# Two half chunks of weights at a time: sixteen wide matmuls, then sixteen narrow ones, in a two-block transformer kernel

## The reference, cut to what matters

```python
def first_block(x, mem, ...):          # per layer
    h = rms_norm(x, norm_mix[l])
    z = h @ w_in[l]                    # 2048 x 5144, then gMLP, dilated and NSA attention
    x = x + jnp.concatenate([out_a, out_b, out_c], axis=-1) @ w_out[l]
    ...
    x = x + o @ xattn_wo[l]            # cross attention to 256 memory tokens
    h = rms_norm(x, norm_mlp[l])
    x = x + jnp.square(jax.nn.relu(h @ w_up[l])) @ w_down[l]      # 2048 x 8192 x 2048
    return rms_norm(x, final_norm)

def second_block(x, c, ctx, ...):
    h_lat = x * (1.0 + sc_m) + sh_m    # modulation, from silu(c) @ w_ada
    mix_lat, _ = _token_mixer(h_lat, h_ctx, ...)   # gated linear attention and pooling, w_in, w_gla_out, w_pool_out, w_out
    x = _layer_norm(DEEPNORM_ALPHA * x + gt_m * mix_lat, ...)
    ffn_lat = _swiglu(x * (1.0 + sc_f) + sh_f, w_ffn_in, w_ffn_out)   # 2048 x 11264, 5632 x 2048
    return _layer_norm(DEEPNORM_ALPHA * x + gt_f * ffn_lat, ...)
```

## Time and profile before

| | |
|---|---|
| median of 3 runs | 3040.98 us |
| lowest, highest | 3037.58, 3041.06 us |
| span of the profiled execution | 3038.4 us |
| PE busy | 2968.7 us (98%), 16590 matmuls |
| DVE busy | 2176.0 us (72%) |
| ACT busy | 1460.2 us (48%) |
| HBM read | 635.52 MB, 213 GB/s over the span |

### The profile page before, as it was taken

The page is one execution under the profiler, slowest core; times in us unless marked ns, Lnnn a source line. Parts: engine busy times, 40 slices in busy tenths (PEclk is TensorE's granted clock), DMA queues, the critical chain, the costliest instruction groups (busy, mean ns, idle before and its releaser), DMA issues.

```text
span 3038.4 us, 40261 instructions
## 1 busy us (share of the span) xinstructions
PE 2968.7 (98%) x16590; PEld 2552.0 (84%) x16590; DVE 2176.0 (72%) x2685; ACT 1460.2 (48%) x1953; POOL 8.5 (0%) x21
## 2 busy tenths in 40 slices
PE   8999999999999999999999999999999999999998
PEld 7888888888888888877887778888878888888887
DVE  5556767899899886677766666648888775555557
ACT  5345555544444445444544444544546444444444
POOL 0000000000000000000000000000000000000000
PEclk9999999999999999999999999999999999999999
DMA  6545244677677785566654445559556765555553
GB/s 250 194 166 207 99 139 143 235 272 260 249 273 265 289 314 197 192 230 241 248 211 171 171 168 190 202 217 345 215 179 232 287 244 193 187 188 192 184 193 111
DMA packets 106661, 648.60 MB, mean 213 GB/s; under 512 B 11856, under 2 KB 11856, under 8 KB 42352
## 3 DMA queue, kind: packets, MB, share of 16 engines
q1 hardware_dynamic: 99936, 621.86, 56.5%
q10 hardware_dynamic: 4608, 16.78, 1.4%
q0 software_dynamic: 1936, 7.41, 0.7%
HBM read 635.52 MB, written 10.49 MB: 213 GB/s over the span
## 4 chain that ended last, share of the span: by engine, by line
PE 92%; DVE 5%; ACT 2%; issue 1%; DMA 1%; SPq 0%; DVEq 0%; ACTq 0%
PE PS L510 50%; PE PS L515 26%; PE PS L551 3%; PE PS L553 3%; PE PS L558 3%; DVE RL L2084 1%; PE PS L1081 1%; PE PS L993 1%; PE PS L788 1%; ACT RH L1226 1%; PE PS L927 0%; PE PS L973 0%; DMA RW<-in_w_ckv 0%; PE PS L579 0%; PE PS L690 0%
## 5 line engine op out<-in xcount | busy, mean ns | idle before, releaser
L2084 DVE TENSOR_TENSOR RL<-RW,RH 128x1024 fp32r<-128x1024 f32 x974 | 1178.1, 1221 | 559.2 <-ACT RH L1226 552.7
L1226 ACT ACTIVATE RH<-RW 128x1024 fp32r<-128x1024 f32 x974 | 1015.5, 1055 | 780.8 <-PE PS L515 634.0
L510 PE MATMUL PS<-A,RH 128*128 128x512 f32 x4544 | 1163.4, 398 | 26.4 <-ACT RH L1226 10.1
L510 PEld LDWEIGHTS PS<-A,RH 128*128 128x128 f32 x4544 | 825.9, 191 | 188.3 <-issue 31.6
L515 PEld LDWEIGHTS PS<-A,RL 128*128 128x128 f32 x4544 | 624.8, 192 | 45.5
L515 PE MATMUL PS<-A,RL 128*128 128x256 f32 x4544 | 637.6, 283 | 0.0
L510 PE MATMUL PS<-H,RH 128*128 128x512 f32 x2304 | 581.9, 394 | 1.2 <-ACT RH L1226 1.2
L510 PEld LDWEIGHTS PS<-H,RH 128*128 128x128 f32 x2304 | 415.9, 189 | 76.7 <-issue 1.4
L515 PEld LDWEIGHTS PS<-H,RL 128*128 128x128 f32 x2304 | 314.7, 191 | 22.7
L515 PE MATMUL PS<-H,RL 128*128 128x256 f32 x2304 | 321.5, 282 | 0.0
L1233 ACT ACTIVATE LT<-PS 128x512 f32<-128x512 f32 x232 | 138.2, 596 | 326.9 <-PE PS L515 326.8
(11 more groups left out here) (256 smaller groups left out, 1560.0 us busy)
## 6 DMA issues: line engine op xcount, KB each, us to landing
RW<-in_w_fin SPq DMA_DIRECT2D x88, 1024.0 KB, 4.8
G<-in_w_ada SPq DMA_DIRECT2D x160, 512.0 KB, 5.9
RW<-in_w_up SPq DMA_DIRECT2D x64, 1024.0 KB, 4.9
RW<-in_w_down SPq DMA_DIRECT2D x64, 1024.0 KB, 5.1
RW<-in_w_fout SPq DMA_DIRECT2D x44, 1024.0 KB, 4.8
RW<-in_w_v SPq DMA_DIRECT2D x32, 1024.0 KB, 4.8
RW<-in_w_bg SPq DMA_DIRECT2D x32, 1024.0 KB, 4.8
RW<-in_w_k SPq DMA_DIRECT2D x16, 1024.0 KB, 4.8
```

The lines of the kernel that those rows point to most:

```text
L510: t.matmul(pair[mm][:, :], wh[:, k, mm * 128:mm * 128 + 128], x2(4 * c + k)[0], start=first and k == 0, stop=False, skip_group_check=True)
L1226: a.activation(m.high(x), m.slot(j)[:, x % 2 * HC:x % 2 * HC + HC], ACT.Copy).then_inc(s["hi"], 1)
L2084: v.tensor_tensor(m.low(x), m.slot(j)[:, x % 2 * HC:x % 2 * HC + HC], m.high(x).bitcast(F32), ALU.subtract).then_inc(s["lo"], 1)
```

## The change

In the calls of `outb`, `up`, `down`, `g2`, `pout`, `fin`, `fout` and `out2` (616 of the 974 halves) `gemm` gets `paired=True`: on each even turn it lists the wide matmuls of two halves, then the narrow ones of both; on the odd turn it lists no matmul of its own. The loop around it (the `beside` steps, the `yield`s, the other lanes) is as before. `outa`, `gout`, `xq` and the rest keep one half at a time. In all products the last wide matmul of a half raises a new semaphore `hused`, and ScalarE, before it overwrites a high buffer, waits for `hused` and `lo` of the half that lay there instead of `used`. What SyncE and the evacuations wait for is unchanged.

```diff
-        for b, c in steps(blocks, halves, zipped):
-            n = num.half
-            num.half += 1
+
+        def high(n, b, c):
+
             if c == 0:
                 block_begins(g0 + b)
             t.wait_ge(s["hi"], n + 1)
...
                 for mm in range(2):
-                    t.matmul(pair[mm][:, :], wh[:, k, mm * 128:mm * 128 + 128], x2(4 * c + k)[0], start=first and k == 0,
-                             stop=False, skip_group_check=True)
+                    done = t.matmul(pair[mm][:, :], wh[:, k, mm * 128:mm * 128 + 128], x2(4 * c + k)[0],
+                                    start=c == 0 and k == 0, stop=False, skip_group_check=True)
+            done.then_inc(s["hused"], 1)
+
+        def low(n, b, c):
+
             t.wait_ge(s["lo"], n + 1)
...
             done.then_inc(s["used"], 1)
+
+        order = steps(blocks, halves, zipped)
+        for x, (b, c) in enumerate(order):
+            n = num.half
+            num.half += 1
+            last = c == halves - 1
+            if not paired:
+                high(n, b, c)
+                low(n, b, c)
+            elif x % 2 == 0:
+                high(n, b, c)
+                high(n + 1, *order[x + 1])
+                low(n, b, c)
+                low(n + 1, *order[x + 1])
             if rest is not None:
                 next(rest, None)
             yield
...
             if x >= NR:
-                a.wait_ge(s["used"], x - NR + 1)
+                a.wait_ge(s["lo"], x - NR + 1)
+                a.wait_ge(s["hused"], x - NR + 1)
             a.activation(m.high(x), m.slot(j)[:, x % 2 * HC:x % 2 * HC + HC], ACT.Copy).then_inc(s["hi"], 1)
```

More of the change, by code:

```diff
@@ L105 @@
 SIGNALS = (
-    "hi", "lo", "used", "cmp", "lt",
+    "hi", "lo", "hused", "used", "cmp", "lt",
     "sil", "fh", "fl", "sq", "sqa", "rs",
@@ L489, in block_begins, with gemm @@
             t.wait_ge(m.pair[g % 2], g // 2)
-    def gemm(blocks, halves, x2, need, zipped=False, beside=None):
+    def gemm(blocks, halves, x2, need, zipped=False, beside=None, paired=False):
         rest, g0 = None, num.block
         num.block += blocks
-        for b, c in steps(blocks, halves, zipped):
-            n = num.half
-            num.half += 1
+        def high(n, b, c):
             if c == 0:
@@ L502, in gemm @@
             wh = m.high(n).rearrange("p (k n) -> p k n", k=4)
-            wl = m.low(n).rearrange("p (k n) -> p k n", k=4)
-            first, last = c == 0, c == halves - 1
             pair = m.banks[2 * ((g0 + b) % 2):2 * ((g0 + b) % 2) + 2]
@@ L509, in gemm @@
                 for mm in range(2):
-                    t.matmul(pair[mm][:, :], wh[:, k, mm * 128:mm * 128 + 128], x2(4 * c + k)[0], start=first and k == 0,
-                             stop=False, skip_group_check=True)
+                    done = t.matmul(pair[mm][:, :], wh[:, k, mm * 128:mm * 128 + 128], x2(4 * c + k)[0],
+                                    start=c == 0 and k == 0, stop=False, skip_group_check=True)
+            done.then_inc(s["hused"], 1)
+        def low(n, b, c):
             t.wait_ge(s["lo"], n + 1)
+            wl = m.low(n).rearrange("p (k n) -> p k n", k=4)
+            pair = m.banks[2 * ((g0 + b) % 2):2 * ((g0 + b) % 2) + 2]
             for k in range(4):
@@ L515, in gemm @@
                     done = t.matmul(pair[mm][:, 0:256], wl[:, k, mm * 128:mm * 128 + 128], x2(4 * c + k)[1], start=False,
-                                    stop=last and k == 3, skip_group_check=True)
+                                    stop=c == halves - 1 and k == 3, skip_group_check=True)
             done.then_inc(s["used"], 1)
+        order = steps(blocks, halves, zipped)
[11 more added lines that the diff above has]
+                low(n + 1, *order[x + 1])
             if rest is not None:
@@ L552, in gemm_n @@
                                  skip_group_check=True)
-                        t.matmul(out[mm], lo(2 * c + k)[:, rows[mm]], wh[:, k, :], start=False, stop=False,
-                                 skip_group_check=True)
+                        done = t.matmul(out[mm], lo(2 * c + k)[:, rows[mm]], wh[:, k, :], start=False, stop=False,
+                                        skip_group_check=True)
+                done.then_inc(s["hused"], 1)
                 t.wait_ge(s["lo"], n + 1)
@@ L578, in small @@
             for k in range(8):
-                t.matmul(bk.ap[:, :], wh[:, k, :], A2(8 * half + k)[0], start=half == k == 0, stop=False,
-                         skip_group_check=True)
+                done = t.matmul(bk.ap[:, :], wh[:, k, :], A2(8 * half + k)[0], start=half == k == 0, stop=False,
+                                skip_group_check=True)
+            done.then_inc(s["hused"], 1)
             t.wait_ge(s["lo"], n + 1)
@@ L871, in mix_of @@
         return need
[L873 removed]
+    L.outb = lambda: gemm(8, 2, twin(m.A, 8), mix_of(4), paired=True)
     L.fed_rest = lambda: None
@@ L931, in up @@
         first = q == b0 == 0
-        yield from gemm(2 * nb, 4, A2, fed(2) if first else nothing, zipped=first)
+        yield from gemm(2 * nb, 4, A2, fed(2) if first else nothing, zipped=first, paired=True)
     def down(q):
-        yield from gemm(8, 4, twin(m.H, 16 * q, 24), lambda c: t.wait_ge(s["ul"], 8 * q + c + 1))
+        yield from gemm(8, 4, twin(m.H, 16 * q, 24), lambda c: t.wait_ge(s["ul"], 8 * q + c + 1), paired=True)
     L.ada, L.up, L.down = ada, up, down
@@ L1149, in tensor_program @@
     L.p2, L.pool = p2, pool
-    L.g2 = lambda: gemm(8, 4, A2, nothing)
+    L.g2 = lambda: gemm(8, 4, A2, nothing, paired=True)
     L.gout = lambda: gemm(8, 4, H2, lambda c: t.wait_ge(s["gl"], c + 1))
-    L.pout = lambda: gemm(8, 2, A2, lambda c: t.wait_ge(s["pl"], c + 1))
+    L.pout = lambda: gemm(8, 2, A2, lambda c: t.wait_ge(s["pl"], c + 1), paired=True)
     L.cp_loads = lambda: idle(12)
@@ L1197, in fin @@
         first = b0 == 0
-        yield from gemm(2 * nb, 4, A2, (lambda c: t.wait_ge(s["fl2"], c + 1)) if first else nothing, zipped=first)
+        yield from gemm(2 * nb, 4, A2, (lambda c: t.wait_ge(s["fl2"], c + 1)) if first else nothing, zipped=first, paired=True)
     def fout(part, first, n):
         yield from gemm(8, n // 4, twin(m.H, first, 24), lambda c: t.wait_ge(s["fgl"], first // 2 + c + 1),
-                        beside=normed(1) if part == 2 else None)
-    L.out2 = lambda: gemm(8, 4, H2, lambda c: t.wait_ge(s["ml2"], 17 + c), beside=normed(0))
+                        beside=normed(1) if part == 2 else None, paired=True)
+    L.out2 = lambda: gemm(8, 4, H2, lambda c: t.wait_ge(s["ml2"], 17 + c), beside=normed(0), paired=True)
     L.modulated_ffn, L.fin, L.fout = modulated_ffn, fin, fout
```

1 line of the change is left out of this document (removed).

## The result

| | before | after |
|---|---|---|
| median of 14 runs each | 3039.44 us | 3034.7 us |
| lowest, highest | 3036.91, 3041.06 us | 3032.11, 3037.44 us |
| span of the profiled execution | 3038.4 us | 3034.1 us |

The ratio of the runs is 0.9984, 95% interval [0.9977, 0.9992]: 4.7 us faster, which is 0.16% and so mostly within the 0.2% named as "no change", to which the prediction gave 0.35 against 0.59 for faster. The forecast of 3033.2 us lies 1.5 us off and its range holds the time, but the saving is 4.7 us where 7.8 were forecast. Half of that miss doesn't show in the time, by luck: the forecast started from a median of 3040.98 us (3 runs), and the same kernel's median over 14 runs is 1.5 us lower. The interval of the ratio is a saving of 2.4 to 7.0 us, so the times only just tell the miss. The traces, one execution of each kernel, show where it is.

What follows compares the result with a forecast made beforehand. TensorE, busy 98% of the span, was taken as the bound. Savings of 5.0 + 3.9 + 1.7 less losses of 1.8 and 0.95 gave 7.8 us, so 3040.98 - 7.8 = 3033.2 us; range 3028.5 to 3038.8 us.

Steps and rivals of the forecast that it cites:

- Part 1, the width: Paired products: each of 308 pairs saves one change from narrow back to wide, 0.018 us each; 5.0 us saved.
- the extra stays: Rival, chance 0.20: pairing doesn't remove the extra 0.018 us per half, so only the other terms count; 3038.2 us.
- The rest, at nothing: Other waits, `w_ada` transposes and earlier buffer release beside attention: no net effect, 1 us allowed either way for the release.
- Parts 2 and 3, `out2`: Block 0's sum one half later, stop and slow clock go, 3.9 us saved; partial sums into idle time, 1.7 saved.
- Part 4, last `fout`: A pair crosses blocks, so VectorE's read-out and the sum over block 0 come later; 1.8 us lost, clock taken as nothing.
- Part 5, start of `fin`: The wait at half (0,3) now precedes narrow matmuls that filled it; 0.95 us lost, stop grows to 2.2 us.
- the new stops let the clock fall: Rival, chance 0.15: at the last `fout` and the start of `fin`, 1.6 us more lost each; 3036.4 us.
- Part 5, start of `up`: The same 0.95 us is lost, but ScalarE's earlier copies bring activations about 0.95 sooner; 0, between -1 and +1.

Runs made afterwards that it cites:

- transposes_early: The changed kernel with TensorE's transposes for the first group of `w_ada` listed one turn earlier; 3032.43 us, 0.9978 of the kernel before.
- sums_moved: The kernel before, unpaired, old release, with `out2`'s sum over block 0 one half later and its partial sums behind the last half; 3033.58 us.
- zip_fout: The changed kernel with the first eight halves of `up` and `fin` unpaired, last `fout` pairs kept within a block, transposes one turn earlier; 3026.25 us.
- no_up_down: The changed kernel without pairs in `up` and `down`; 3029.99 us, 0.9971 of the kernel before.
- pair_only: The changed kernel with all its pairs, but ScalarE waits for `used` as before; 3048.39 us, 1.0037 of the kernel before.
- release_sums: The kernel before plus the early release of high buffers and the moved sums of `out2`, without any pairs; 3029.76 us.
- quads_again: The changed kernel, first eight halves of `up`, `fin` unpaired, last `fout` pairs within blocks, transposes earlier, four halves grouped in `fin` and two `fout`; 3023.72 us.

## Why the prediction was right, and where it was wrong

**Part 1, the width: the mechanism right, its yield not.** The term was 0.018 us per pair; 89.39 - 89.07 over sixteen pairs gives 0.020, fours give 0.020 per change saved, and the 159 pairs with nothing else at them brought 3.2 us for 2.9. The place was right too: only the first five wide spacings of a pair in after are long, 0.232 us, and the other ten are 0.227. The rival "the extra stays" falls. The loss is in `up` and `down`: +0.95 instead of -1.7.

**The rest, at nothing: this step failed, twice.** "It has the time in all but the first `down`" was said of VectorE and the transposes of `w_ada`. It had not: 3.73 us of waiting at 767.66 came back as stops of 0.60 and 1.64 us on TensorE, 82 and 106 us later, and moving the transposes removed them (`transposes_early`). The argument counted when the transposes would come and didn't ask what a wait there would do to VectorE's low parts and ScalarE's high parts behind it. And the release of the high buffers was priced at +-1 us, with the reason that the stops end on chains that don't wait for a buffer. At least one does: the stop at 1326.77 is 0.9 us shorter with the release alone. (At the start of `up` part 5 had seen the path, ScalarE's order with a high copy ahead of the activation work, and its size, 0.95 for 0.9.) The release alone is worth 4 to 6 us; without it pairs lose 9.3, so beside pairs it is worth 13.7. The two errors had opposite signs, and the base was 1.5 us too high: that the time came out 1.5 us from the forecast is luck in good part.

**Parts 2 and 3, `out2`: right,** 4.0 and 2.0 us for 3.9 and 1.9 with the pairs' share, and shown apart from the pairs (`sums_moved`). One thing under part 2 is softer than it was told: of the 3.9 us the 1.56 for the clock are paid in some executions only (14.43 or 16.02 us for the block).

**Part 4, last `fout`: right,** 1.8 us, no fall of the clock in after; `zip_fout` removes it.

**Part 5, start of `fin`: the term of the order right, its clock wrong.** From the arrival of the activations, 18.14 us into `fin` in both traces, before needed 8.54 us to the ninth half, after 11.92. Of the 3.38 us between them 0.95 is the forecast one, eight narrow matmuls that now come behind the wait. The other 2.4 us is the clock that fell behind a stop of 2.41 us, right behind another of 0.72. The prediction allowed that ("up to 1.6 us more, taken as nothing") and as the rival "the new stops let the clock fall", and chose against it with a stop of 1.26 us that left no trace. But its own sum gave a stop of 2.2 us there, next to the 2.30 us that did let it fall. That row was the nearer one. The rival was right at this place, and wrong at the last `fout`. Its price, taken from one half of `out2`, was too small: behind the eight wide matmuls (3.56 us for 1.84) the sixteen narrow ones of the pair were slow as well (2.79 us for 1.91). Nor is this fall that of one execution alone: it stands at this stop in all four traces that have it (after, `transposes_early`, `no_up_down`, `pair_only`; 2.40 to 2.42 us).

**Part 5, start of `up`: inside its bound,** +0.43 for 0 +-1, but by another sum: the stop there was 2.04 us for 1.94 (at 553.85), the clock fell behind it for a second time (0.50 in the window from 555 to 557 us), and against that the slow stretch at the start was shorter.

**What stays open.** The last row of the first table, -1.8 us, is 1.6 ahead of `up`, most of it (1.43) in the product with `w_qc`, where both kernels have the same order. The two runs of the release alone differ by 2.6 us in this same product (70.03 and 72.64 us), so it is taken as the scatter of single executions; what makes it was not tried. Of the 6.0 us between `release_sums` and `quads_again` the traces give 5.5 in stretches that repeat: 3.8 between the ninth half of `fin` and the end, 0.8 in `up` and `down`, and 0.9 in `outb`, `g2`, `pout` and `out2`. Where the release's gain beyond 2.3 us lies, and why the median of `zip_fout` is above the sum of its mends, stays open.

## What to carry to other kernels

Before pricing a reordering on the bounding engine at "no stop, no cost", look at how far each helper engine runs ahead of it at that place: a wait of 3.7 us on VectorE, which took nothing of it back in the next 80 us, came back as 2.2 us of stops on TensorE about a hundred microseconds later. Release a buffer when its last reader is through, even where the engine that waits for it looks idle, if its queue holds other work behind that wait. And when a change moves many things, run its parts alone: here the part that gave the change its name (pairs) cost about 5 us as it stood, hidden by the two that came with it, and was worth 6 us once its stops were mended.

## What the runs showed of the chip

The same stop lets the clock fall in one execution and not in the next (2.15 us in `out2`, 3.02 us ahead of `up`), each time worth about 1.6 us, so there a clock row of one trace is a chance and not a price. At the stop of 2.41 us in `fin` it fell in all four traces that have it. And the eight halves at that place gave 26.7 us in all ten traces that take them singly, whatever the clock did behind the 4.79 us of idle: the stop at (0,3) ends with VectorE's chain, and it swallows what TensorE lost or won ahead of it. A change between 256 and 512 moving columns and back costs 0.020 us, with runs of 8, 16 or 32 narrow matmuls alike (89.39, 89.07 and 88.91 us for 32 halves), and 974 more semaphore increments sixteen or eight matmuls apart cost nothing that 32 halves could show to 0.01 us (89.38 us with them, 89.39 without).
